# MoE combine of an encoder trunk: two rounded matmul passes with a 0/1 matrix in place of one fp32 matmul, gates applied at the addition to the residual

## What is computed

```python
logits = (t @ router_w).astype(jnp.float32)
top_v, top_i = lax.top_k(logits, TOP_K)
top_w = jax.nn.softmax(top_v, axis=-1)
gates = jnp.sum(jax.nn.one_hot(top_i, N_EXPERTS) * top_w[..., None], axis=1)
out = jnp.zeros((B * L, D), jnp.float32)
for e in range(N_EXPERTS):
    out = out + gates[:, e:e + 1] * swiglu(t, w_gate[e], w_up[e], w_down[e])
```

## Time and profile before

| | us |
|---|---|
| three runs | 1754.22, 1754.67, 1757.03 |
| median | 1754.67 |
| the profiled execution: its span | 1756.1 |
| busy in it: PE, DVE, ACT | 1682.2, 1306.9, 1031.5 |
| MoE stage in it, from the first slab to the last add | 745.8 to 1748.2 |
| one pass of it | 124.88 |

### The profile page before, as it was taken

The page is one execution under the profiler, slowest core; times in us unless marked ns, Lnnn a source line. Parts: engine busy times, 40 slices in busy tenths (PEclk is TensorE's granted clock), DMA queues, the critical chain, the costliest instruction groups (busy, mean ns, idle before and its releaser), DMA issues.

```text
span 1756.1 us, 23184 instructions
## 1 busy us (share of the span) xinstructions
PE 1682.2 (96%) x8662; PEld 1426.2 (81%) x8662; DVE 1306.9 (74%) x1111; ACT 1031.5 (59%) x900; POOL 18.3 (1%) x25
## 2 busy tenths in 40 slices
PE   6999999999997799799999999999999999999997
PEld 5998879998886588688878888888888788788785
DVE  6773645544565565588888888888888888988885
ACT  5342435543334443477767677677677677677673
POOL 1000000000000000000000000000000000000000
PEclk9997999999999899899999999999999999999999
DMA  8651535655553043689999999999879899899992
GB/s 308 210 175 52 188 96 170 190 174 195 173 202 120 1 140 142 220 310 365 351 348 366 350 340 371 323 363 375 318 286 366 317 363 376 316 379 341 340 375 114
DMA packets 222433, 461.42 MB, mean 263 GB/s; under 512 B 7314, under 2 KB 52580, under 8 KB 222388
## 3 DMA queue, kind: packets, MB, share of 16 engines
q1 hardware_dynamic: 221696, 459.53, 73.7%
q0 software_dynamic: 528, 1.22, 0.3%
q10 hardware_dynamic: 164, 0.04, 0.0%
HBM read 459.72 MB, written 1.05 MB: 262 GB/s over the span
## 4 chain that ended last, share of the span: by engine, by line
issue 59%; PE 34%; DVE 4%; ACT 2%; POOL 0%; DMA 0%; ACTq 0%; DVEq 0%; POOLq 0%
PE ps L1350 14%; PE ps L1336 13%; PE ps L1498 3%; PE ps L1459 1%; PE ps L1426 1%; PE ps L1445 1%; DVE w_lo L362 1%; ACT ta L659 1%; PE ps L1416 1%; DVE mx L1059 0%; DVE ta L1075 0%; POOL rstd L480 0%; DVE a_lo L792 0%; ACT a_hi L533 0%; DMA rows<-in_ev_conv_w 0%
## 5 line engine op out<-in xcount | busy, mean ns | idle before, releaser
L362 DVE TENSOR_TENSOR w_lo<-raw,w_hi 128x2048 fp32r<-128x2048 f32 x431 | 981.7, 2290 | 261.4 <-ACT w_hi L358 259.9
L358 ACT ACTIVATE w_hi<-raw 128x2048 fp32r<-128x2048 f32 x431 | 826.6, 1919 | 409.2 <-PE ps L1601 138.3
L1601 PE MATMUL ps<-w_hi,e_hi 128*128 128x512 f32 x896 | 354.2, 395 | 2.8 <-DVE e_lo L1201 2.8
L1601 PE MATMUL ps<-w_hi,e_lo 128*128 128x512 f32 x896 | 349.6, 390 | 0.0
L1601 PE MATMUL ps<-w_lo,e_hi 128*128 128x512 f32 x896 | 349.0, 389 | 0.0
L1601 PEld LDWEIGHTS ps<-w_hi,e_hi 128*128 128x128 f32 x896 | 168.3, 188 | 36.2 <-issue 3.0
L1601 PEld LDWEIGHTS ps<-w_hi,e_lo 128*128 128x128 f32 x896 | 168.2, 188 | 35.9
L1601 PEld LDWEIGHTS ps<-w_lo,e_hi 128*128 128x128 f32 x896 | 168.4, 188 | 33.5
L1623 PE MATMUL ps<-w_hi,at_hi 128*128 128x512 f32 x448 | 175.7, 392 | 1.9 <-DVE at_lo L1213 1.9
L1623 PE MATMUL ps<-w_lo,at_hi 128*128 128x512 f32 x448 | 175.1, 391 | 0.0
L1623 PE MATMUL ps<-w_hi,at_lo 128*128 128x512 f32 x448 | 174.9, 390 | 0.0
(11 more groups left out here) (273 smaller groups left out, 1701.4 us busy)
## 6 DMA issues: line engine op xcount, KB each, us to landing
raw<-in_moe_w_up SPq DMA_DIRECT2D x112, 1024.0 KB, 7.0
raw<-in_moe_w_gate SPq DMA_DIRECT2D x110, 1024.0 KB, 6.9
raw<-in_moe_w_down SPq DMA_DIRECT2D x110, 1024.0 KB, 6.5
raw<-in_xa_wkv SPq DMA_DIRECT2D x16, 1024.0 KB, 5.1
raw<-in_ev_w_in SPq DMA_DIRECT2D x14, 1024.0 KB, 8.6
raw<-in_od_w_in SPq DMA_DIRECT2D x12, 1024.0 KB, 5.1
raw<-in_ffd_w_gate SPq DMA_DIRECT2D x11, 1024.0 KB, 5.3
raw<-in_ffd_w_up SPq DMA_DIRECT2D x11, 1024.0 KB, 5.4
```

Of the source, the lines that this page charges most:

```text
L358: nc.scalar.activation(w_hi[:, n % CUT, :], at_, ACT.Copy).then_inc(hi_cut, 1)
L362: nc.vector.tensor_tensor(w_lo[:, n % CUT, :], place(n, r, behind)[0], w_hi[:, n % CUT, :].bitcast(F32), ALU.subtract).then_inc(lo_cut, 1)
L1601: mm = T.matmul(ps[:, bank, :], s, m, start=(h == 0 and k == 0 and j == 0), stop=(h == 1 and k == 3 and j == 2))
```

## The change

ACT rounds y from PSUM into `y_hi` (`y_up`, new), placed after the high cut of G0 + 1 and before that of G0 + 2 (after the last pass it stands alone). DVE's copy of y becomes a subtraction that writes `y_lo`, and it waits for `y_up`. `pgate` and its semaphore go; PE transposes `pack` instead, so `spread` holds 0 and 1, in fp32r. `combine` issues two fp32r matmuls (y_hi, y_lo) where it had one in fp32. The adds to X become scalar_tensor_tensor instructions that multiply by the gate; the column of the gate is read from a table in SBUF into a register (`column`, L1195) before them.

```diff
@@ -150,6 +150,9 @@
         a_hi = sb("a_hi", [P, KT, 256], F32R)
         a_lo = sb("a_lo", [P, KT, 256], F32R)
         ta = sb("ta", [P, 2048])
+        with ExitStack() as s:
+            sb("tb_front", [P, D], F32, s)
+            y_lo = sb("y_lo", [P, D], F32R, s)
         tb = sb("tb", [P, 2048])
         rot = sb("rot", [P, 2, 512])
         const = sb("const", [P, 3 * P + 56])
@@ -193,9 +196,9 @@
             e_sig = sb("e_sig", [P, 512], F32, s)
             e_act = sb("e_act", [P, 512], F32, s)
             pack = sb("pack", [P, 2, BLK], F32, s)
-            pgate = sb("pgate", [P, 2, BLK], F32, s)
-            spread = sb("spread", [P, 2 * P], F32, s)
-            y = sb("y", [P, D], F32, s)
+            spread = sb("spread", [P, 2 * P], F32R, s)
+            y_hi = sb("y_hi", [P, D], F32R, s)
+            sb("e_spare", [P, 2 * BLK], F32, s)
             ones = sb("ones", [P, P], F32, s)
             lg = sb("lg", [P, 12, 16], F32, s)
             pos16 = sb("pos16", [P, 2, 16], F32, s)
@@ -275,7 +278,7 @@
         packed, e_ps, e_h, e_l = sem("packed"), sem("e_ps"), sem("e_h"), sem("e_l")
         g_sig, act_rdy = sem("g_sig"), sem("act_rdy")
         at_ps, at_h, at_l = sem("at_ps"), sem("at_h"), sem("at_l")
-        pg_rdy, pg_ps, pg_t = sem("pg_rdy"), sem("pg_ps"), sem("pg_t")
+        pg_ps, pg_t, y_top = sem("pg_ps"), sem("pg_t"), sem("y_top")
         y_sb, c_ps, x_half, combined, out_rdy, out_done = (sem(n) for n in (
             "y_sb", "c_ps", "x_half", "combined", "out_rdy", "out_done"))
 
@@ -727,11 +730,19 @@
                 cut_hi(act, G0 + 4, i, behind)
                 cut_hi(act, G0 + 5, i, behind)
 
+            def y_up(q):
+
+                act.wait_ge(slab_used, G0 + PASS + PASS * q)
+                nc.scalar.activation(y_hi[:, :], ps[:, 2:4, :].rearrange("p a n -> p (a n)"),
+                                     ACT.Copy).then_inc(y_top, 1)
+
             def a_next(q, behind):
 
                 cut_hi(act, G0, 7 * q, behind)
                 pack_hi(q)
-                for n in range(1, 6):
+                cut_hi(act, G0 + 1, 7 * q, behind)
+                y_up(q - 1)
+                for n in range(2, 6):
                     cut_hi(act, G0 + n, 7 * q, behind)
 
             def a_pass(q, spans):
@@ -752,6 +763,7 @@
             with act.Fori(HP + 1, n_pass) as q:
                 a_next(q, True)
                 a_pass(q, [(1, NB, True)])
+            y_up(n_pass - 1)
             n_fin = 2 + 2 * [n for n in NORMS if n not in ("ret", "dif")].index("fin")
             for t in range(2):
 
@@ -1213,25 +1225,17 @@
                 V.tensor_tensor(at_lo[:, :, :], shaped(ps[:, 4, :], 4), at_hi[:, :, :].bitcast(F32),
                                 ALU.subtract).then_inc(at_l, 1)
 
-            def add_pass(done):
+            def add_pass(done, col):
 
                 for t in range(2):
                     b0 = 6 if t == 0 else 2
                     dve.wait_ge(c_ps, 2 * done + t + 1)
-                    V.tensor_tensor(X[:, t, :], ps[:, b0:b0 + 2, :].rearrange("p a n -> p (a n)"), X[:, t, :],
-                                    ALU.add).then_inc(x_half if t == 0 else combined, 1)
-
-            def pack_gates(col):
-
-                for t in range(2):
-                    p_, g_ = ((a[:, t, col:col + 1] if isinstance(col, int) else a[:, t, bass.ds(col, 1)])
-                              for a in (pos16, gate16))
-                    ins = V.tensor_scalar(pgate[:, t, :], slot, p_, g_, ALU.is_equal, ALU.mult)
-                ins.then_inc(pg_rdy, 1)
+                    V.scalar_tensor_tensor(out=X[:, t, :], in0=ps[:, b0:b0 + 2, :].rearrange("p a n -> p (a n)"),
+                                           scalar=gate16[:, t, bass.ds(col, 1)], in1=X[:, t, :], op0=ALU.mult,
+                                           op1=ALU.add).then_inc(x_half if t == 0 else combined, 1)
 
             cut_lo(dve, G0 + 2)
             pack_lo(0)
-            pack_gates(0)
             for n in range(3, 6):
                 cut_lo(dve, G0 + n)
 
@@ -1248,8 +1252,9 @@
                 cut_lo(dve, G0 + 5, i, behind)
 
             def v_y(q):
-                dve.wait_ge(slab_used, G0 + PASS + PASS * q)
-                V.tensor_copy(y[:, :], ps[:, 2:4, :].rearrange("p a n -> p (a n)")).then_inc(y_sb, 1)
+                dve.wait_ge(y_top, q + 1)
+                V.tensor_tensor(y_lo[:, :], ps[:, 2:4, :].rearrange("p a n -> p (a n)"), y_hi[:, :].bitcast(F32),
+                                ALU.subtract).then_inc(y_sb, 1)
 
             def v_next(q, behind):
 
@@ -1263,12 +1268,11 @@
             def v_pack(q):
                 col = column(q)
                 pack_tokens(col)
-                pack_gates(col)
 
             def v_pass(q, spans, pack_more):
                 e_mul(7 * q, 2)
                 with dve.If(q > 0) if not isinstance(q, int) else nullcontext():
-                    add_pass(q)
+                    add_pass(q, column(q - 1))
                 dve.wait_ge(pg_ps, q + 1)
                 V.tensor_copy(spread[:, :], ps[:, 5, 0:256]).then_inc(pg_t, 1)
                 with dve.If(pack_more) if pack_more is not None else nullcontext():
@@ -1289,7 +1293,7 @@
                 v_next(q, True)
                 v_pass(q, [(1, NB, True)], q < n_pass - 1)
             v_y(n_pass - 1)
-            add_pass(n_pass)
+            add_pass(n_pass, column(n_pass - 1))
 
             dve.wait_ge(in_fin, 16)
             dve.wait_ge(n_sq, 2 + 2 * sum(n not in ("ret", "dif") for n in NORMS))
@@ -1632,8 +1636,9 @@
                 for t in range(2):
                     b0 = 6 if t == 0 else 2
                     for o in range(2):
-                        mm = T.matmul(ps[:, b0 + o, :], spread[:, t * P:(t + 1) * P], y[:, 512 * o:512 * o + 512],
-                                      start=True, stop=True)
+                        for yv in (y_hi, y_lo):
+                            mm = T.matmul(ps[:, b0 + o, :], spread[:, t * P:(t + 1) * P],
+                                          yv[:, 512 * o:512 * o + 512], start=yv is y_hi, stop=yv is y_lo)
                     mm.then_inc(c_ps, 1)
 
             pe.wait_ge(n_out, 2 * (NORMS["moe"] + 1))
@@ -1651,9 +1656,8 @@
                 half_in(G0 + 3, i, 1, 1)
                 with pe.If(q > 0):
                     combine(q - 1)
-                pe.wait_ge(pg_rdy, q + 1)
                 for t in range(2):
-                    mm = T.transpose(ps[:, 5, t * P:(t + 1) * P], pgate[:, t, :], ident)
+                    mm = T.transpose(ps[:, 5, t * P:(t + 1) * P], pack[:, t, :], ident)
                 mm.then_inc(pg_ps, 1)
 
                 for lo_, hi_ in ((1, 2), (2, NB)):
```

## The result

| | before | after |
|---|---|---|
| median of the first runs (4 and 4) | 1755.85 | 1745.45 |
| lowest to highest | 1754.22 to 1757.98 | 1744.07 to 1748.77 |
| span of the profiled execution | 1756.1 | 1743.4 |

The ratio of after to before is 0.9938, with a 95% interval of 0.9923 to 0.9953: some 11 us (8 to 13.5) of 1755. Timed again beside other kernels (six runs, and eleven of before), it was 0.9956 (0.9942 to 0.9970), 5 to 10 us. The forecast was a gain of 10.8 us and a time of 1743.9 us. The median after, 1745.45, is 1.55 above that time, and 1.18 of it is the reference: with its fourth run the median of before is 1755.85 instead of 1754.67.

What follows compares the result with a forecast made beforehand. PE's list of work was taken to set the pace: seven transitions saving 1.61 less a 0.10 stall, plus 0.2 at the end, gave 10.8 us and 1743.9 us. The range was 1741.3 to 1748.4 us.

Steps and rivals of the forecast that it cites:

- What bounds the kernel: MoE stage: PE never waits, so work taken from its list comes off the time if supplies still arrive.
- The combine: PE between passes: eight fp32r matmuls at 0.227 us replace 3.43 us of fp32 rows, saving 1.61 us each.
- The stall at G0 + 2: After each transition: `y_up` delays the cuts, so PE's weight load comes late; 0.1 us, bounds 0 and 0.31.
- The slack at G0 + 6: DVE's low cut for that slab ends 0.13 us before PE, now sooner, wants it: stall 0.
- The loads: Raw slabs by DMA: 357 GB/s wanted, 373 seen; almost 4 us of cover, cost 0.
- The end: After the last pass, everything on the path: 6.24 us becomes 6.05, a gain of 0.2 if PE's clock stays up.
- the first four matmuls: Final combine, ahead of the first add: 3 × 0.227 + 0.48 + 0.05 = 1.21 us.
- The rival of a fallen clock: Final combine: matmuls at 0.427 us after longer PE idle, end 1.04 us slower than now, 1745.1 us; chance 0.23.
- The sum: Whole kernel: 7 × (1.61 − 0.10) + 0.2 = 10.8 us gained, giving 1743.9 us.
- no stall: Rival for the transitions: 7 × 1.61 + 0.2 = 11.5 us gained, 1743.2 us; shares the forecast's chance of 0.50.
- The slower rival: Transitions: `y_up` over 3.2 us uses up the saving; at 4 us, about 1763 us; chance 0.04.
- a side argument: PE's weight loads: a late one is partly absorbed, since weights are normally loaded one matmul (0.23 us) ahead.

Runs made afterwards that it cites:

- the gates alone: Kernel before with only the gates moved to the adds, y still one fp32 copy and fp32 combine: 0.9992 of before, all six passes 124.88 us.
- the doubled `y_up`: Changed kernel with a second ACT copy of y out of PSUM, into an unused buffer, ahead of `y_up`: a pass of 124.30 us.
- y behind G0 + 2: Changed kernel with `y_up` and `v_y` moved behind the high and low cuts of G0 + 2: passes 123.28 and 123.29 us, ratio to before 0.9940.
- the put-back work: Changed kernel with the two removed `pgate` instructions put back on DVE behind `pack`, into an unused buffer: a pass of 123.72 us.
- y_hi only: Changed kernel with the `y_lo` matmuls of the combine left out, so the sum lacks the rest of y: a pass of 123.23 us.
- split end: Changed kernel with `y_up`, `v_y` behind the cuts of G0 + 2 and the last pass's y handled in 512-column halves: passes 123.27 to 123.30 us, ratio 0.9941.
- both parts on DVE: Changed kernel with y rounded and subtracted on DVE, nothing of y on ACT: passes of 124.34 to 124.39 us.

## Why the prediction was right

- **What bounds the kernel**: PE's list of work. Held in all profiles. Wherever its list was left alone the pass was 124.88; where it was shortened, the pass followed until a low cut was late.
- **The combine**: 1.61 us forecast (8 × 0.227 for 3.43), 1.62 measured. DVE's changed parts made none of it: the gates alone left the pass at 124.88.
- **The stall at G0 + 2**: 0.1 forecast. By the pass, 1.62 − 1.49 = 0.13; by what the reordering gives back, 0.10. The steps behind it came out nearly as written: `y_up` 1.03 (1.04), the cut 0.93 later (0.93), the low cut 0.29 later (0.31), `v_y` not delayed.
- **The slack at G0 + 6**: 0.13 forecast, 0.22 measured, no stall. The two adds were 1.28 each as forecast, but take 2.38 together where the sum had 2.47, because the second no longer waits and overlaps the first. The table read is hidden: the first add follows the product by 0.60 us (1002.81 to 1003.41).
- **The loads**: free, as forecast. 357 GB/s, and no wait for a raw slab.
- **The end**: 0.2 forecast, 0.1 measured, with full clock. The term that was too small is that of the first four matmuls: 1.21 forecast, 1.33 measured (1731.55 to 1732.88), as the second starts 0.33 us after the first and not 0.23. The rival of a fallen clock was not seen in the two profiles of the changed kernel, but in three others with the same end or a longer one (the doubled `y_up`, y behind G0 + 2, the put-back work): the two adds, 1.20 us apart at full clock, stand 1.72 or 1.73 apart there, since the combine feeds them slower. From the start of `y_up` to the end of the second add it is 7.30 us in the first of them, where the clock is low for the whole combine (the rival's sum was 7.28), and 6.75 and 6.68 in the others, where it falls during the combine; at full clock it is 6.15. So the condition on which the forecast of the end rested held in the profiles by luck, and up to 1.15 us hung on it.
- **The sum**: 10.8 us forecast, 10.6 by the profile (10.5 in transitions, 0.1 at the end), 10.4 by the first medians. The interval, 8 to 13.5 us, would also hold the sums with no stall (11.5) or with a fallen clock at the end (9.5); it is the pass of 123.39 us that says which terms were right. The step from a span of 1756.1 us to a median 1.4 lower compares unlike things: where both are recorded, a run's time is 1.8 to 2.3 us above its span. The gain doesn't rest on it. The slower rival needed a `y_up` of over 3.2 us; it took 1.03.

What failed was a side argument. I took it that a late weight load is always partly absorbed; that depends on what PE does ahead of it.

## What to carry to other kernels

In a kernel whose busiest engine never waits, price an edit by that engine's rows, start to start, and then look for the few places where the suppliers have less slack than the edit takes. An average idle share of 12% or 25% says nothing about them: here 0.92 us more on an engine idle for a quarter of the pass cost 0.915. Where a faster step uses slack elsewhere, look for work to take off that other engine in the same change; measured alone such work looks worthless.

## What the hardware showed that was not expected

**The clock at the end comes and goes.** All kernels have the same idle time of 1.86 or 1.87 us ahead of the last down slabs. In the profiles of six (before, y_hi only, `y_up` twice, y behind G0 + 2, put-back work, split end) the granted clock fell to the lower level (1.2 GHz) behind it; in four (the changed kernel twice, gates alone, both parts on DVE) it didn't. In the kernels with `y_up` on ACT that is the difference between 8.6 us and 7.0 us of ACT's idle time ahead of it, 1.6 us of the time. The y-behind-G0 + 2 kernel, right behind the idle time:

```profile
1724.50:1727.90 3.40, 3.40 (x9) 2.68 (x10) 0.00 (x0) 0.00 (x0) 0.00 (x0) 0.55 0.00 0
```

The second fall, at the final combine, goes with the first. Six kernels issue eight fp32r matmuls behind an idle time of 2.37 us or more. The three that had the first fall (`y_up` twice, y behind G0 + 2, put-back work) had the second too, with a granted clock of 0.54 to 0.75 over the combine; the three without the first (the changed kernel twice, both parts on DVE) kept full clock. Behind shorter idle times (1.32 us in before, 1.51 in the split end) the clock stayed up in spite of the first fall, and so it did over the four matmuls of y_hi only, behind 2.37 us. In ten profiles this is a pattern and not a cause; what decides whether the clock falls was not tried.

**The stretch ahead of the MoE stage varies more than the change's details.** It is the same program in all, and the long issue link starts between 725.0 us (y_hi only) and 730.3 us (gates alone). That is why differences of a microsecond had to be read from passes and not from times. What makes it vary was not tried.
